# Causal mask of an attention stage: from a TensorE product with the identity to an addition on VectorE

## The reference, cut to what matters

```python
def one_block(args):                       # q_blk: 128 queries of each head
    q_blk, blk = args
    s = jnp.einsum('bqhd,bkhd->bhqk', q_blk, k).astype(jnp.float32)
    qpos = blk * Q_BLOCK + jnp.arange(Q_BLOCK)
    s = jnp.where(kpos[None, :] <= qpos[:, None], s, -jnp.inf)
    p = jax.nn.softmax(s, axis=-1).astype(v.dtype)
    return jnp.einsum('bhqk,bkhd->bqhd', p, v)
```

## Time and profile before

| what | us |
|---|---|
| median of three runs (3463.04 to 3470.42) | 3463.91 |
| time of the profiled execution | 3470.39 |
| its span, first to last instruction | 3468.6 |
| PE busy in the span | 3142.5 (91%) |
| DVE busy in the span | 1245.4 (36%) |
| attention stage, first score work to the copy of the last output | 248 to 495 |

### The profile page before, as it was taken

The page is one execution under the profiler, slowest core; times in us unless marked ns, Lnnn a source line. Parts: engine busy times, 40 slices in busy tenths (PEclk is TensorE's granted clock), DMA queues, the critical chain, the costliest instruction groups (busy, mean ns, idle before and its releaser), DMA issues. The chain is left out here.

```text
span 3468.6 us, 42498 instructions
## 1 busy us (share of the span) xinstructions
PE 3142.5 (91%) x14871; PEld 1722.7 (50%) x14872; DVE 1245.4 (36%) x3058; ACT 882.1 (25%) x1714; POOL 580.0 (17%) x1035
## 2 busy tenths in 40 slices
PE   8969889868896999999799999999989969988886
PEld 6536654368443444444356666666644434333332
DVE  5865554465343212222423333223212241122224
ACT  1022224324221111111234444444420011111111
POOL 0000010066011112211311111111110001122223
PEclk9979999978898999999899999999989989999998
DMA  7910001132318979995701111110031168899975
GB/s 294 352 49 1 0 13 36 42 83 62 106 52 364 373 315 402 424 402 233 280 31 37 37 37 37 37 37 1 1 129 37 37 269 326 330 427 424 413 318 223
DMA packets 182210, 612.93 MB, mean 177 GB/s; under 512 B 55194, under 2 KB 106133, under 8 KB 149047
## 3 DMA queue, kind: packets, MB, share of 16 engines
q1 hardware_dynamic: 150998, 566.46, 42.0%
q0 software_dynamic: 22080, 42.01, 3.2%
q10 hardware_dynamic: 8992, 2.62, 0.3%
HBM read 592.59 MB, written 53.00 MB: 186 GB/s over the span
## 5 line engine op out<-in xcount | busy, mean ns | idle before, releaser
L1907 PE MATMUL ret_pqkv<-ret_w,hT_mix 128*128 128x512 f32 x1024 | 452.2, 595 | 1.9 <-PEq L2647 1.9
L2480 PE MATMUL f0e_pgu<-f0w_gu,f0e_xT 128*64 128x512 f32 x1568 | 345.9, 595 | 8.3 <-issue 4.5
L1769 PE MATMUL mo_py<-mo_w,mixT 128*128 128x512 f32 x768 | 335.2, 597 | 5.5 <-DMA mo_w<-in_hy_w_out_dram 3.0
L2480 PE MATMUL f1e_pgu<-f1w_gu,f1e_xT 128*64 128x512 f32 x1344 | 296.8, 597 | 7.4 <-issue 3.6
L1907 PEld LDWEIGHTS ret_pqkv<-ret_w,hT_mix 128*128 128x128 f32 x1024 | 190.4, 191 | 218.0 <-issue 217.9
L2480 PEld LDWEIGHTS f0e_pgu<-f0w_gu,f0e_xT 128*64 128x64 f32 x1568 | 144.6, 138 | 203.1 <-issue 183.2
L1769 PEld LDWEIGHTS mo_py<-mo_w,mixT 128*128 128x128 f32 x768 | 146.0, 192 | 187.6 <-issue 178.9
L1915 PE MATMUL ret_pgate<-ret_w,hT_mix 128*128 128x256 f32 x1024 | 231.6, 379 | 0.0
L2499 PE MATMUL f1e_pd<-f1w_d,f1e_hidT 128*64 128x512 f32 x672 | 167.4, 649 | 43.3 <-DMA f1w_d<-in_moe_w_down_dram 41.5
L1915 PEld LDWEIGHTS ret_pgate<-ret_w,hT_mix 128*128 128x128 f32 x1024 | 189.6, 190 | 23.6 <-issue 0.5
L2480 PEld LDWEIGHTS f1e_pgu<-f1w_gu,f1e_xT 128*64 128x64 f32 x1344 | 103.8, 138 | 195.3 <-issue 195.2
(11 more groups left out here) (556 smaller groups left out, 4594.5 us busy)
## 6 DMA issues: line engine op xcount, KB each, us to landing
f0w_gu<-in_moe_w_gate_dram SPq DMA_DIRECT2D x32, 2048.0 KB, 11.0
f0w_gu<-in_moe_w_up_dram SPq DMA_DIRECT2D x32, 2048.0 KB, 16.6
f0w_d<-in_moe_w_down_dram SPq DMA_DIRECT2D x64, 1024.0 KB, 12.9
f1w_gu<-in_moe_w_gate_dram SPq DMA_DIRECT2D x32, 2048.0 KB, 15.6
f1w_gu<-in_moe_w_up_dram SPq DMA_DIRECT2D x32, 2048.0 KB, 25.6
f1w_d<-in_moe_w_down_dram SPq DMA_DIRECT2D x64, 1024.0 KB, 14.1
mixT<-in_ada_w_dram SPq DMA_DIRECT2D x80, 512.0 KB, 5.9
ret_w<-in_ret_w_in_dram SPq DMA_DIRECT2D x16, 1024.0 KB, 9.5
```

The costliest lines, as they stand in the source:

```text
L1769: mm = pe.matmul(py[t % 3][:, half * 512:(half + 1) * 512], mixT[:, kk, t * P:(t + 1) * P], ws[:, kk, half * 512:(half + 1) * 512], start= ...
L1907: mm = pe.matmul(p_qkv[s % 2][:, :], g.hT[:, kk, t * P:(t + 1) * P], w[h % 2][:, kk, 0:512], start=(kk == 0), stop=(kk == KD - 1))
L2480: mm = pe.matmul(pgu[s][half * HALF:(half + 1) * HALF, :], xT[u % 2][:, kk, s * HALF:(s + 1) * HALF], ew.gu[u][:, :, kk, half * FH:(half + ...
```

## The change

The product of the identity with `futureT` is gone from `scores`. `top` now begins with an addition on VectorE that reads the diagonal block of `at_s` and `futureT` and writes the sum over the block in PSUM. The row maximum waits for it on a new semaphore, `masked`. Every product of L879 now ends its group by itself (`stop=True`), and the last one signals `scored`.

```diff
@@ scores
                 for c0 in range(0, end, 512):
                     c1 = min(c0 + 512, end)
-                    pe.matmul(s[:, c0:c1], qT[u][:, i * P:end], kT[u][:, c0:c1], start=True, stop=(c1 < end))
-
-                pe.matmul(s[:, i * P:end], g.ident[:, :], g.futureT[:, :], start=False, stop=True).then_inc(scored, 1)
+                    mm = pe.matmul(s[:, c0:c1], qT[u][:, i * P:end], kT[u][:, c0:c1], start=True, stop=True)
+                mm.then_inc(scored, 1)
@@ top
                 dve.wait_ge(scored, m * NI + n + 1)
+                own = sc[n % 2][:, i * P:(i + 1) * P]
+                dve.tensor_tensor(own, own, g.futureT[:, :], ALU.add).then_inc(masked, 1)
+                dve.wait_ge(masked, m * NI + n + 1)
                 dve.tensor_reduce(tot[:, n:n + 1], sc[n % 2][:, 0:(i + 1) * P], AX.X, ALU.max).then_inc(topd, 1)
                 dve.wait_ge(topd, m * NI + n + 1)
                 dve.tensor_scalar(nmax[:, n:n + 1], tot[:, n:n + 1], -MLA_SCALE, None, ALU.mult).then_inc(maxed, 1)
```

More of the change, by code:

```diff
@@ L842, in attention @@
         po = [g.ps(ctx, f"at_po{u}", [P, 512]) for u in range(2)]
-        (w_in, krok, staged, kd, qd, kok, qok, scored, maxed, probs, turned, pTok, pv, topd, invd, normed, oTd, oTok) = g.sems(
+        (w_in, krok, staged, kd, qd, kok, qok, scored, maxed, probs, turned, pTok, pv, topd, invd, normed, oTd, oTok,
+         masked) = g.sems(
             ctx, "at", "w_in", "krok", "staged", "kd", "qd", "kok", "qok", "scored", "maxed", "probs", "turned", "pTok",
-            "pv", "topd", "invd", "normed", "oTd", "oTok")
+            "pv", "topd", "invd", "normed", "oTd", "oTok", "masked")
         block = g.stage(ctx)
```

## The result

The changed kernel takes 3481.18 us (median of 6 runs, 3476.49 to 3483.34) against 3466.05 of the kernel before in the same measurement (6 runs, 3456.27 to 3470.53). The ratio is 1.004, with a 95% interval from 1.0024 to 1.0055: about 15 us slower, outside the range of the prediction and on the other side of the forecast. The two groups of runs do not overlap. The profiled execution took 3480.96 us.

A forecast was written before the change was run, and what follows sets the result against it. TensorE was taken to bound the attention stage, with VectorE late at four places a pass. Saving 0.85 us a pass, 3.4 us in four, from the 3463.91 us median gave 3460.5 us, range 3453 to 3469.

The forecast's parts named there:

- What bounds the stage: Attention stage: TensorE leads through most items, VectorE is late at four places a pass; stage change reaches program end whole.
- The prices at full clock: Attention items: mask product 0.22 us off TensorE; addition 0.29 us plus 0.03 us to the row maximum on VectorE.
- the question that the prediction left between 242 and 449 ns: Cost of one VectorE addition with output in PSUM: taken as 0.29 us, bounds 242 and 449 ns.
- The walk: Both engines' streams followed through the second attention pass: a pass 0.85 us shorter, four passes 3.4 us.
- Seven additions on the path: VectorE in each pass: additions of items 0, 2 or 3, 4, 7, 10, 11 and 15 count, 0.32 us each.
- moving each start to the later of the engine's turn and the release, with the steps of the rows: Method for timing both streams of the second attention pass from the old profile's steps; gave 0.85 us less a pass.
- the clock falls: Rival: clock falls at PV(7) or PV(15), up to 1.5 us more at one place of a pass; 10 in 100.
- both places: Case of the clock rival: falls at PV(7) and PV(15) of each pass, +12 less 3.4 us, 3472.
- VectorE leads everywhere: Rival: all 64 additions paid at 0.32 us, every mask gained; +5.6 us, 3469.5, up to 3480; 8 in 100.

The follow-up runs named there:

- the filled passes: Kernels before and after, each with and without mask product or addition, with unread identity products in TensorE's waits; passes 57.91, 55.47, 59.77 and 57.76 us.
- e3: Kernel before with its mask products kept and the change's additions put in as well; 3482.07 us, ratio 1.0045.
- e6: Kernel after with unread products of the identity with itself only at the start of each pass's items; 3460.91 us, ratio 0.9982.

## Why the prediction was wrong, by its own steps

- **What bounds the stage** was read rightly: TensorE, and VectorE at four places of a pass. The stage's end did shift all that follows, which is as long as before (2973.5 and 2972.4 us).
- **The prices at full clock** held: 298 ns for the addition (0.29 taken), 0.03 us to the row maximum, 0.22 us for a product. The 298 ns with output in PSUM against 292 in SBUF closes the question that the prediction left between 242 and 449 ns.
- **The walk** had the right waits: 1.01, 0.51, 1.24 and 0.78 us against 1.0, 0.5, 1.2 and 0.9, with one more at PV(9) that makes 15.8 us in 20 waits against 14 to 15 in 16. Seven additions on the path is what the filled passes show (2.29 us). The sum was mis-sized even so: -0.85 us a pass, measured -0.15 at full clock. 0.21 of that is the product of S(2) at low clock, which the kernel after did save (in the pass shown PV(0) comes 0.32 us earlier, 0.33 forecast) and the filled ones can't. The rest is VectorE: at full clock it leads in items 1 and 2, and in the filled kernels PV(1) comes 0.2 us later after the change, not 0.46 earlier.
- **The step that failed** is "moving each start to the later of the engine's turn and the release, with the steps of the rows". These steps carry the clock of the kernel before with them, so a change of the clock stood in the sum at nothing; it was only a rival of 10 in 100. The runs show in its place some 49 us more at 1.2 GHz (34 to 83) and a stage 13.3 us longer instead of 3.4 shorter. In the pass shown the walk holds up to PV(0); PV(2) comes at +0.97 us from S(0) instead of -0.27, and PV(15) at +1.18 instead of -0.85 and then takes 1.7 us more.
- **The rival *the clock falls*** was the right mechanism. It had the place PV(15) and a price of 1.5 us for one place of a pass. It lacked the start of the items, where the change takes two products out of a stretch in which TensorE does little already (wait before T(0) 0.57 us before, 1.12 after) and where filling is worth most. By its own rows ("both places", 3472, which is 8.6 over the median it started from) it fell 6.5 us short of the 15.1 measured. That it had the place PV(15) right and PV(7) wrong is in part luck: nothing in the kernel before told which wait would bring the fall.
- **The rival *VectorE leads everywhere*** gave 3469.5 for an addition of 0.29 us. Its mechanism fell: 16 additions on the path would be 5.1 us a pass, the filled kernels show 2.29 and 1.86.

The Trainium skill, TensorE: Matmul & The Clock Gate, section "HAM oscillation — how this bites in real kernels", describes a clock that falls again in every wait for a tile. The runs here agree that the falls recur from pass to pass, PV(15) with its 3.68 us for 2.00 first. The waits that it describes are DMA waits longer than the work between them, some 2 us there; the ones near the falls here are only 0.5 to 1.4 us long.

What stays open: which wait brings a fall and why it lasts 3 us in one pass and over 6 in another. In the kernel before, too, low stretches at the start of the items differ from pass to pass (3 to 6 us). In e3 TensorE waits 0.90 us before T(0) in the second pass and keeps full clock, so that wait alone does not bring the fall. And e6 shows that filling one place moves the falls at others.

## What to carry to other kernels

A product of TensorE that fills a gap may be worth more than its time: before you take work off TensorE, look at the granted clock around its waits, and price low clock (here 0.3 to 0.4 us for each microsecond) as a term of the sum, not as a mishap. To compare two variants by their work, bring both to full clock first with products into unused columns; and where such filling stands in waits, keep it.

## What the runs showed that I had not expected

Two edits that each leave the mean clock of the stage at 0.93 and 0.91 bring it to 0.84 together, because they lower it at different places. And 96 products that nobody reads made the kernel after 21 us faster; 132 with 12 of them ahead of the stage made it 25 us faster, with a granted clock of 1.00 over the whole stage.
